# A router on the raw residual, and another order of the mixers' output projection, in a two-layer hybrid trunk on one core

## The reference, cut to what matters

```python
for l in range(2):
    mix = hybrid_mixer(x, ...)                    # four pooling groups | four mLSTM heads, joined, @ w_out[l]
    h = layer_norm(ALPHA * x + mix, ln1_g[l], ln1_b[l])
    f = swiglu(h, ...) if l == 0 else moe_swiglu(h, ...)
    x = layer_norm(ALPHA * h + f, ln2_g[l], ln2_b[l])

def moe_swiglu(x, w_router, b_router, wg, wu, wd):
    logits = x @ w_router + b_router              # 8 experts
    top_v, top_i = lax.top_k(logits, 2)
    ...                                           # softmax of the two, each expert's swiglu, weighted sum
```

## Time and profile before

| | |
|---|---|
| median of 3 runs | 1279.82 us (1277.58 to 1280.05) |
| profiled execution | 1277.31 us, of which the span is 1275.3 us |
| TensorE busy | 1231.2 us, 97% of the span |
| VectorE busy | 765.6 us, 60% |
| ScalarE busy | 595.3 us, 47% |
| GpSimd busy | 92.2 us, 7% |
| moved by DMA | 425.07 MB, mean 333 GB/s |
| granted TensorE clock | 0.994 of full speed over the span |

### The profile page before, as it was taken

The page is one execution under the profiler, slowest core; times in us unless marked ns, Lnnn a source line. Parts: engine busy times, 40 slices in busy tenths (PEclk is TensorE's granted clock), DMA queues, the critical chain, the costliest instruction groups (busy, mean ns, idle before and its releaser), DMA issues.

```text
span 1275.3 us, 16103 instructions
## 1 busy us (share of the span) xinstructions
PE 1231.2 (97%) x6391; PEld 888.5 (70%) x6391; DVE 765.6 (60%) x817; ACT 595.3 (47%) x572; POOL 92.2 (7%) x109
## 2 busy tenths in 40 slices
PE   8989999999999999999999999999999999999996
PEld 7987888887987866665656666756665666666662
DVE  5888654457888757546545546655653555565643
ACT  5555444345454455455434445545544444456521
POOL 1661000000570000000000000000000000000000
PEclk9999999999999999999999999999999999999999
DMA  9737655554435789999999999999999999999994
GB/s 313 284 102 239 216 182 196 190 174 143 150 116 206 289 353 388 420 419 419 419 408 420 420 419 419 419 419 403 419 419 420 418 420 411 419 419 420 419 418 189
DMA packets 88496, 425.07 MB, mean 333 GB/s; under 512 B 9520, under 2 KB 11856, under 8 KB 76128
## 3 DMA queue, kind: packets, MB, share of 16 engines
q1 hardware_dynamic: 87056, 420.21, 83.2%
q0 software_dynamic: 1216, 3.71, 1.1%
q10 hardware_dynamic: 144, 0.07, 0.0%
HBM read 422.91 MB, written 1.05 MB: 332 GB/s over the span
## 4 chain that ended last, share of the span: by engine, by line
PE 69%; DVE 11%; DMA 10%; issue 4%; ACT 4%; SPq 1%; DVEq 0%; ACTq 0%
PE bank L1784 16%; PE bank L1785 15%; PE bank L1786 15%; PE bank L2165 10%; PE bank L2159 7%; DMA raw<-in_wu_exp 3%; DVE w_lo L1183 3%; DMA raw<-in_wg_exp 2%; DVE arena L1287 1%; DMA arena<-in_wd_exp 1%; DMA work<-in_wd_exp 1%; DVE w_lo L1206 1%; DMA raw<-in_wd_exp 1%; ACT w_hi L840 1%; PE bank L2120 1%
## 5 line engine op out<-in xcount | busy, mean ns | idle before, releaser
L1183 DVE TENSOR_TENSOR w_lo<-raw,w_hi 128x1792 fp32r<-128x1792 f32 (+1 forms) x131 | 273.5, 2104 | 176.0 <-ACT w_hi L840 165.9
L1784 PE MATMUL bank<-w_hi,parts 128*128 128x512 f32 x888 | 340.9, 384 | 16.2 <-DVE w_lo L1183 11.6
L1785 PE MATMUL bank<-w_lo,parts 128*128 128x512 f32 x888 | 334.4, 377 | 0.0
L1786 PE MATMUL bank<-w_hi,parts 128*128 128x512 f32 x888 | 333.5, 376 | 0.0
L840 ACT CAST w_hi<-raw 128x1792 fp32r<-128x1792 f32 (+1 forms) x131 | 229.3, 1762 | 133.1 <-DMA raw<-in_wg_exp 52.4
L1784 PEld LDWEIGHTS bank<-w_hi,parts 128*128 128x128 f32 x888 | 167.8, 189 | 68.5 <-issue 32.4
L1786 PEld LDWEIGHTS bank<-w_hi,parts 128*128 128x128 f32 x888 | 167.3, 188 | 31.8
L1785 PEld LDWEIGHTS bank<-w_lo,parts 128*128 128x128 f32 x888 | 168.1, 189 | 29.0
L1206 DVE TENSOR_TENSOR w_lo<-raw,w_hi 128x2048 fp32r<-128x2048 f32 x60 | 138.6, 2311 | 59.7 <-PE bank L1786 46.3
L860 ACT CAST w_hi<-raw 128x2048 fp32r<-128x2048 f32 x60 | 114.0, 1910 | 74.9 <-PE bank L1786 65.7
L2165 PE MATMUL bank<-raw,arena 128*64 128x512 f32 (+1 forms) x720 | 140.6, 542 | 0.0
(11 more groups left out here) (270 smaller groups left out, 1245.6 us busy)
## 6 DMA issues: line engine op xcount, KB each, us to landing
raw<-in_wg_exp SPq DMA_DIRECT2D x92, 896.0 KB, 14.7
raw<-in_wd_exp SPq DMA_DIRECT2D x78, 1024.0 KB, 15.8
raw<-in_wu_exp SPq DMA_DIRECT2D x89, 896.0 KB, 15.4
arena<-in_wu_exp SPq DMA_DIRECT2D x26, 896.0 KB, 14.3
arena<-in_wd_exp SPq DMA_DIRECT2D x22, 1024.0 KB, 17.2
arena<-in_wg_exp SPq DMA_DIRECT2D x24, 896.0 KB, 15.0
raw<-in_w_in SPq DMA_DIRECT2D x20, 1024.0 KB, 5.8
work<-in_wd_exp SPq DMA_DIRECT2D x12, 1024.0 KB, 16.4
```

The source lines that it names most:

```text
L1183: v.tensor_tensor(low(o)[:, 0:w], ring[s][:, 0:w], high(o)[:, 0:w].bitcast(F32), ALU.subtract) \
L1784: mm(psum, left[0], right[0], start=first, stop=False)
L1785: mm(psum, left[0], right[1], start=False, stop=False)
L1786: return mm(psum, left[1], right[0], start=False, stop=last)
```

## The change

It has these parts.

- **Mixer, silu order.** The last two silus change places (3 before 7), and silu 7 moves behind the copies of the first three pooling inputs. These copies wait for seven silus instead of eight, and GpSimd's pooling now waits for all eight itself.
- **Projection order.** After unit 0 and the heads' turns come unit 1 of both tiles, units 2 and 3 of tile 0, units 2 and 3 of tile 1. The turn of tile 0's rows moves to the middle of tile 1's unit 3 in layer 0, and to the end of tile 1's unit 2 in layer 1. Layer 1's logits of tile 0 come behind the projection.
- **Router.** Norm 3 is taken apart. With r the raw residual, m its mean, s the inverse deviation, g and b the norm's scale and shift, W the router's weights and c its bias, the logits are `s * (r @ (gW) - m * sum(gW)) + (sum(bW) + c)`. GpSimd makes gW and bW in layer 0 (16 small multiplies), TensorE sums them over the channels with a product by ones (`router_sums`), turns the raw residual as each half of it is ready, and multiplies it by gW. ScalarE only copies the turned tile (`router_tile`), both halves, and takes the root behind that. VectorE forms the token rows from the residual with two fused operations (`row_scaled`, `row_shifted`), and of tile 1 the second of them comes behind the choice of experts.
- **Filler products** are 3, 3, 12 and 5 instead of 9, 6, 10 and 8.
- **Queue.** The loads that waited for the logits wait for both tiles' logits by a count of 2; those that wait for the token rows still do.

```diff
-        SILU_ORDER = (0, 1, 4, 5, 2, 6, 7, 3)
+        SILU_ORDER = (0, 1, 4, 5, 2, 6, 3, 7)
...
                 if 0 in groups:
+                    pool.wait_ge(qk_ready, 8 * (l + 1))
                     pool.wait_ge(u_ready, GROUPS * l + 1)
...
                 load_ln(2 * l + 1)
                 if l + 1 < LAYERS:
+                    pool.wait_ge(router_in, 32)
+                    pool.wait_ge(par_ready, 2)
+                    pool.wait_ge(gatew_ready, 2)
+                    for k in range(DK):
+                        for n, gb in enumerate("gb"):
+                            g.tensor_scalar(rout_gb[:, k, n * E:(n + 1) * E], rout_w[:, k, :], par_col((NORM[3][0], gb), 1, k),
+                                            None, ALU.mult).then_inc(routgb_ready, 1)
...
                 silu(6)
-                silu(7)
                 silu(3)
...
-                act.wait_ge(qk_ready, 8 * (l + 1))
+                act.wait_ge(qk_ready, 8 * l + 7)
                 for c in range(GROUPS - 1):
                     pool_input(c)
+                silu(7)
...
+            def router_tile(t):
+                for n in range(2):
+                    act.wait_ge(turned, 2 * (TT * 3 + t) + n + 1)
+                    a.copy(xf[:, t, 4 * n:4 * n + 4, :].rearrange("p k c -> p (k c)"), bank[TURN_BANKS[t][n]]) \
+                        .then_inc(xf_act, 1)
+
+            def router_norm():
+                router_tile(0)
+                norm_std(3, 0)
+                ahead()
+                token_high(0)
+                router_tile(1)
+                norm_std(3, 1)
+                ahead()
...
+            def router_residual(t, n):
+                c = slice(n * HALF, (n + 1) * HALF)
+                dve.wait_ge(*sum_event(3, t, n))
+                v.scalar_tensor_tensor(out=work[:, t, c], in0=tokens[:, t, c], scalar=ALPHA, in1=bank[SUM_BANKS[t][n]][:, :],
+                                       op0=ALU.mult, op1=ALU.add).then_inc(res_ready, 1)
+
+            def router_stats(t):
+                dve.wait_ge(res_ready, 2 * t + 2)
+                for n in range(2):
+                    st.add(v.bn_stats(stats[:, t, n, :], work[:, t, n * HALF:(n + 1) * HALF]))
+                st.wait()
+                v.bn_aggr(mv[:, t, :], stats[:, t].rearrange("p a b -> p (a b)")).then_inc(var_ready, 1)
+                dve.wait_ge(std_ready, TT * 2 + t + 1)
+                dve.wait_ge(var_ready, TT * 2 + t + 1)
+                st.then(v.reciprocal(rstd[:, t, 1:2], rstd[:, t, 0:1]))
...
+            def logit_of(t):
+                dve.wait_ge(logit_mm, TT)
+                st.wait()
+                st.then(v.scalar_tensor_tensor(out=logit[:, t, :], in0=rout_sum, scalar=mv[:, t, 0:1],
+                                               in1=bank[0][:, t * E:(t + 1) * E], op0=ALU.mult, op1=ALU.add))
+                st.add(v.scalar_tensor_tensor(out=logit[:, t, :], in0=logit[:, t, :], scalar=rstd[:, t, 1:2],
+                                              in1=rout_c, op0=ALU.mult, op1=ALU.add))
+
+            for n in range(2):
+                router_residual(0, n)
+            router_stats(0)
+            ahead()
+            row_scaled(0)
+            row_shifted(0)
+            router_residual(1, 0)
+            token_low(0)
+            router_residual(1, 1)
+            dve.wait_ge(routsum_mm, 1)
+            st.add(v.tensor_scalar(rout_sum, bank[2][:, 0:E], -1.0, None, ALU.mult))
+            st.add(v.tensor_tensor(rout_c, bank[2][:, E:2 * E], rout_b[:], ALU.add))
+            router_stats(1)
+            row_scaled(1)
             for t in range(TT):
-                st.add(v.tensor_tensor(logit[:, t, :], bank[0][:, t * E:(t + 1) * E], rout_b[:], ALU.add))
+                logit_of(t)
...
                             TOP_K - 0.5, None, ALU.is_lt).then_inc(chosen_ready, 1)
+            row_shifted(1)
...
-            token_low(1)
...
             wide_picks(lambda t: posm[:, t, 0:1])
-            token_low(0)
+            token_low(1)
...
-                        if (t, q, half) == (1, 2, 0):
+                        if (t, q, half) == ((1, 2, 1) if l else (1, 3, 0)):
                             turn(2 * l + 1, 0)
-                        elif l and (t, q, half) == (1, 3, 0):
+                        elif l and (t, q, half) == (1, 3, 1):
                             logits(0, range(DK))
+                            router_sums()
...
-                for t in range(TT):
-                    for q in range(1, 4):
-                        if t == 0:
-                            arrived(mixer_unit(l, "w", q))
-                        if q == 2:
-                            pe.wait_ge(ylo_ready, 4 * l + 3 + t)
-                        project(q, t)
+                for q, t in ((1, 0), (1, 1), (2, 0), (3, 0), (2, 1), (3, 1)):
+                    if t == 0:
+                        arrived(mixer_unit(l, "w", q))
+                    if q == 2:
+                        pe.wait_ge(ylo_ready, 4 * l + 3 + t)
+                    project(q, t)
...
-            unread(9, bank[1])
+            unread(3, bank[1])
             turn(3, 1)
-            unread(6, bank[1])
-            logits(1, range(DK)).then_inc(logit_mm, 1)
-            unread(10, bank[1])
+            unread(3, bank[1])
+            logits(1, range(DK))
+            unread(12, bank[1])
...
-            unread(8, bank[2])
+            unread(5, bank[2])
```

More of the change, by code:

```diff
@@ L382, in build @@
         n_over_f = on_side([1])
+        rout_sum, rout_c = (on_side([E]) for n in range(2))
         assert at_side[0] <= GATE_W + GATE_RAW + POOL_W
@@ L1028, in _ @@
                 mixer(l)
-                norm(2 * l + 1)
                 if l == 0:
+                    norm(1)
                     dense()
                     norm(2)
+            router_norm()
             token_high(1)
@@ new lines, in row_scaled, with row_shifted @@
+            def row_scaled(t):
+                dve.wait_ge(ln_in, 32 * 3)
+                st.add(v.scalar_tensor_tensor(out=tokens[:, t, :], in0=work[:, t, :], scalar=mv[:, t, 0:1],
+                                              in1=ln_rows[3][:, 0, :], op0=ALU.subtract, op1=ALU.mult))
+            def row_shifted(t):
+                st.wait()
+                v.scalar_tensor_tensor(out=tokens[:, t, :], in0=tokens[:, t, :], scalar=rstd[:, t, 1:2],
+                                       in1=ln_rows[3][:, 1, :], op0=ALU.mult, op1=ALU.add).then_inc(tokens_ready, 1)
@@ new lines, in _ @@
+            dve.wait_ge(tokens_ready, TT * 2)
+            for n in range(2):
+                router_residual(0, n)
+            router_stats(0)
+            ahead()
+            row_scaled(0)
[6 more added lines that the diff above has]
+            st.add(v.tensor_tensor(rout_c, bank[2][:, E:2 * E], rout_b[:], ALU.add))
@@ L1788, in logits, with router_sums @@
             def logits(t, ks):
-                pe.wait_ge(router_in, 32)
                 for k in ks:
                     pe.wait_ge(*xf_event(3, t, k // 4))
-                    last = mm(bank[0][:, t * E:(t + 1) * E], xf[:, t, k, :], rout_w[:, k, :],
+                    last = mm(bank[0][:, t * E:(t + 1) * E], xf[:, t, k, :], rout_gb[:, k, 0:E],
                               start=k == 0, stop=k == DK - 1)
-                return last
+                last.then_inc(logit_mm, 1)
+            def router_sums():
+                pe.wait_ge(routgb_ready, 2 * DK)
+                for k in range(DK):
+                    last = mm(bank[2][:, 0:2 * E], ones, rout_gb[:, k, :], start=k == 0, stop=k == DK - 1)
+                last.then_inc(routsum_mm, 1)
             def turn(s, t):
@@ L1803, in turn @@
                 for k in range(DK):
+                    if s == 3 and k % 4 == 0:
+                        pe.wait_ge(res_ready, 2 * t + k // 4 + 1)
                     last = tr(bank[TURN_BANKS[t][k // 4]][:, (k % 4) * P:(k % 4 + 1) * P],
```

26 lines of the change are left out of this document (11 added, 15 removed).

## The result

The changed kernel takes 1280.65 us (median of 20 runs, 1278.03 to 1283.30), the kernel before 1277.93 us (20 runs on the same chips, 1275.42 to 1280.85). The ratio is 1.0019, 95% interval 1.0012 to 1.0026: slower, by about 2.4 us, where 1278.8 against 1279.82 was forecast. Against the forecast's change of -1.0 us (ratio 0.9992) the result is 3.4 us off, and a ratio of 1 lies outside the interval.

What follows compares the result with a forecast made beforehand. Once the experts run, the DMA queue was taken as the bound, so the end follows the first expert product. -2.0 us there plus +1.0 for the clock gave -1.0: 1278.8 against 1279.82, range 1275.6 to 1281.9.

Steps and rivals of the forecast that it cites:

- the mixer's gain: Mixer, both layers: new silu order and earlier pool inputs win 0.83 to 1.28 us, taken as 1.27.
- the clock: Layer 0's dense start: longer TensorE stands lower the granted clock, at most 1.7 us, taken as +1.0.
- rival 2: Clock falls fully at dense start, router and first expert products: +2.9 us net, 1282.7; chance 0.10.
- a choice later than 415: Layer 1's router: sign of being wrong; the choice of experts was forecast at 413.6, 2.0 us earlier.
- The end moves by as much as the first expert product: Expert stage: the kernel's end shifts exactly as the first expert product does, forecast at 421.3 instead of 423.32.
- late next: Mixer's decay stage: exps and ScalarE's weight rounding come some 1.3 us earlier; VectorE had stood 1.91 us for that rounding.
- the lower bound: Mixer: gain of only 0.83 us if GpSimd's pooling chain, now waiting for all eight silus, starts late.
- no fall in 400 to 425 now: Layer 1's router stretch: the clock did not fall there before, taken as evidence against more clock falls.
- Layer 0's order: Layer 0's projection: stand of 1.38 us filled with 2.75 us of products, mixer's win spent; net +0.1 us.
- The router's chain: Layer 1's router along VectorE: 2.4 us stand for the root, choice at 413.6, first expert product 2.0 us earlier.
- The loads: Queue: four loads waiting for token rows go out at 414.9 instead of 413.54, costing 0, or 1.4 without the hole.
- the hole: DMA rate at 445 to 450 us: 13 GB/s with TensorE full, read as the landing ring being full.

Runs made afterwards that it cites:

- kernel with everything kept busy: Changed kernel with a gate chunk ahead of the weighted scores, 14 dense-start fillers, early router sums, 12 router fillers instead of 3: 1274.4 us, 0.9967.
- cover on both sides: VectorE's second subtraction moved and TensorE's stands filled with work: on the changed kernel 0.9960, on the kernel before (no router fillers) 0.9974.
- the router's fillers: Changed kernel with router sums in tile 1's last unit and 12 fillers instead of 3 before tile 1's turn: 1279.04 us, 1.0005.
- the two best kernels: Changed kernel with subtraction moved and TensorE's stands filled, then nearly the same with layer 0's old projection order: 1273.14 and 1271.55 us.
- the second kernel: Changed kernel with subtraction moved, stands filled (6 dense-start fillers instead of 14) and layer 0's old projection order: 1271.55 us, 0.9944.
- the silus alone: Kernel before with only the new silu order and pool inputs: 1278.03 us, 0.9991.
- the router alone: Kernel before with only the raw-residual router, its filler counts and scaled weights, old silu and projection order: 1278.87 us, 1.0002.
- the dense fillers: Changed kernel with 14 filler products in the three stands of layer 0's dense start, nothing else: 1280.22 us, 1.0015.

## Why the prediction was wrong, by its own steps

Two terms of the sum failed, the mixer's gain and the clock, and rival 2 was given too few places and too small a chance. One of the prediction's own signs of being wrong, a choice later than 415, came: it was at 419.93. Shifts in the profiled execution, as forecast and as measured:

| stretch | forecast | changed kernel | kernel with everything kept busy |
|---|---|---|---|
| layer 0, to the heads' turns | -1.27 | +0.22 | -1.32 |
| heads' turns to dense start | +1.37 | +1.02 | +1.03 |
| dense start to mixer 1 | 0 (clock: +1.0) | +1.56 | -0.01 |
| mixer 1 to its heads' turns | -1.27 | +1.35 | -1.90 |
| heads' turns to first expert product | -0.83 | -0.33 | -1.39 |
| sum | -2.0 (+1.0) | +3.82 | -3.59 |

Of the first row, -0.56 (changed kernel) and +0.19 (kept busy) were there at layer 0's copy of the gates' columns already, ahead of anything that the change touches. Behind the first expert product the changed kernel lost another 1.7 us, to a span 5.5 longer: the fall of the clock at 445 to 450, where TensorE was full. "The end moves by as much as the first expert product" left that out.

1. **The mixer's term, 1.27 us a layer: the step that failed first.** The copies did leave the stand before the pooled inputs (no stand there now), and the scores come earlier. I had written that VectorE's rounding wait is "late next" and would come earlier too, and named as the lower bound only GpSimd's pooling. I didn't follow GpSimd one step further, to the masks that the weighted scores wait for. With the exps earlier, masks and subtraction start together (364.39 and 364.40), the masks take 3.27 us instead of 1.22, and the weighted scores' products start only 0.86 us (layer 0) and 0.26 us (layer 1) earlier, counted from the copy of the gates' columns, where 1.27 was forecast: 1.4 us short over both layers. These products then ran at half clock, 1.64 and 1.48 us longer, which took the rest and more; that part is the clock's, the next step. Moving the subtraction behind the weighted scores, and nothing else, gave 4.1 us of medians back. The contention itself stood in the earlier trace rows, and I used it to price the 16 small multiplies (which cost nothing, rightly) and not the masks. The Trainium skill (GPSIMD Engine Reference, Key points) names it for VectorE instructions with two SBUF inputs, which the subtraction has; the masks at 3.27 beside it and 1.22 alone agree.
2. **The clock's term, +1.0 at one place: mis-sized.** At the dense start it fell as forecast (118.51, first product 0.77 us) and took 1.56 us in the profile. But it fell in both weighted scores, in the router and in the first experts too. Time at half clock went from 19 to 32.7 us. Over the runs of one and the same kernel, the time rises 0.28 us for each us at half clock (14 kernels together, each against its own mean), so 13.7 us are worth 3.9 us: more than the whole loss of 2.4 to 2.7. At equal clock the change would be worth about -1.2 to -1.5 us, by an estimate from that slope. Measured with cover on both sides it is 0.9960 against 0.9974, -1.8 us (the intervals overlap, and only the first has fillers in the router), near the -2.0 of the sum without the clock.
3. **Rival 2** had the mechanism and three of its places (dense start, router, first experts; the weighted scores were missing) and was set at 0.10, since I took "no fall in 400 to 425 now" as evidence against. It was weak evidence: the change takes 10 filler products out there, and with 12 in place of 3 and the sums elsewhere the clock held at 1.00 through the router. By its own rule it "decides once all three fall for their full length"; in the profiled execution they did, and that one took 1282.62 us where the rival said 1282.7. That closeness is luck: the weighted scores' falls and the masks' delay are not in its sum.
4. **Layer 0's order**, "nothing: +0.1 us": right as arithmetic (+1.09 measured at the turn for the 1.37 between the stand and the products), wrong as a net, since only 0.86 of the 1.27 that was to pay for it came, and the fall of the clock took that too.
5. **The router's chain** was right, as long as the clock held. VectorE stood 2.21 us for the root (2.4 forecast). From the turn of tile 0 to the first expert product I had 23.95 us, and with the router's fillers it took 23.68 (399.03 to 422.71). The changed kernel took 24.75, as long as before (24.78), at half clock for part of it: the choice came at 419.93, 17.5 us behind that turn, against 16.25 forecast.
6. **The loads** that wait for the token rows went out at 421.15 instead of 413.54 and cost nothing: the hole behind them is whole, and TensorE stood only 0.23 us for an expert weight there (0.21 before). Of what the two best kernels gain up to the first expert product, 0.8 to 2.0 us are lost again by the last products (-3.53 to -2.74 and -4.91 to -2.90). TensorE was full there, and a fall of the clock lies near 440 us in both (the second kernel's granted clock is 0.87 over 435 to 440 and 0.79 over 440 to 445); that the fall alone takes it was not tested.

What stays open: which execution falls at which of these places. The kernel before got through a stand of 1.77 us at full clock in its own profile and the silus alone through one of 2.30, the router alone fell after 1.77, and the dense fillers moved falls rather than removing them. So the time of one fall can't be assigned to one edit from single profiles, only the total over runs.

## What to carry to other kernels

When an edit lets one engine run earlier, follow each thing that starts earlier to the engine beside which it will now run, here GpSimd's masks beside VectorE's subtraction; the remedy was to move one instruction behind the work that TensorE waits for. Price a filler product as what holds the clock, and treat "the clock doesn't fall here" as a fact about the present schedule with its fillers. Removing a stand of TensorE gains only if the work that fills it isn't ahead of the chain that sets the next stage.

## What the runs showed of the hardware

- The spread of one kernel's times goes with its clock. The changed kernel's seven runs at a mean granted clock of 0.989 average 1279.2 us, the one at 0.984 took 1283.3; the kernel before averages 1280.7 us at 0.989 or 0.990 (11 runs) and 1276.9 at 0.994 (18). A straight line through clock and time explains 0.78 of the variance in the changed kernel and 0.40 in the kernel before.
- Two masks of 128x512 took 1.22 us with VectorE standing and 3.27 us with its subtraction (128x2048) beside them, and the subtraction took 2.77 instead of 2.28 us: both engines pay.
- The clock fell in stretches in which TensorE was busy by the profile: 5.00 of 5.00 us in 410 to 415 (clock 0.50) and in 445 to 450 (0.66). The first fall began in a run of 32 products of 8 and 16 columns from 406.00 on: over 406 to 408 the clock was 1.00, over 408 to 410 0.62. The Trainium skill (TensorE: Matmul & The Clock Gate, The HAM clock gate) ties the clock to how busy the engine has recently been; the busy share in the profile doesn't show that for these two windows.
